# Norm boundaries: squares added on TensorE, residual terms for two blocks at once, modulation sums moved into the mixer

## What is computed

```python
c_act = jax.nn.silu(c)
for i in range(DEPTH):                          # DEPTH = 2
    mod = c_act @ ada_w[i] + ada_b[i]           # ada_w[i]: 1024 x 6144
    sh1, sc1, g1, sh2, sc2, g2 = jnp.split(mod[:, None, :], 6, axis=-1)
    h = rmsnorm(x, norm_g[i, 0]) * (1.0 + sc1) + sh1
    y = mlstm_mixer(h, ...) if i == 0 else sgu_mixer(h, ...)
    x = x + g1 * rmsnorm(y, norm_g[i, 1])
    h = rmsnorm(x, norm_g[i, 2]) * (1.0 + sc2) + sh2
    y = jnp.square(jax.nn.relu(h @ ffn_w1[i])) @ ffn_w2[i]
    x = x + g2 * rmsnorm(y, norm_g[i, 3])
```

## Time and profile before

| | us |
|---|---|
| median of 3 runs | 2249.4 |
| lowest, highest | 2245.52, 2251.71 |
| the profiled execution | 2242.23 |
| its span | 2240.4 |
| PE busy in it | 2130.8 |
| VectorE, ScalarE, POOL busy | 1230.7, 825.4, 96.0 |

### The profile page before, as it was taken

How to read it: one execution, slowest core, us unless ns; L and a number is a source line. 1 busy time by engine, 2 the same in 40 slices (tenths; PEclk the granted TensorE clock), 3 DMA queues, 4 the chain that set the end, 5 groups by cost and what they waited for, 6 DMA issues and landing times.

```text
span 2240.4 us, 29806 instructions
## 1 busy us (share of the span) xinstructions
PE 2130.8 (95%) x11614; PEld 1780.1 (79%) x11614; DVE 1230.7 (55%) x1994; ACT 825.4 (37%) x1229; POOL 96.0 (4%) x71
## 2 busy tenths in 40 slices
PE   6999879999998999999999999998989999999997
PEld 5897778888888998788888888884666689888886
DVE  4665766666667345647333336425557756536455
ACT  3433334334234222325242343334445534324243
POOL 0000010000001002401000000100000000000000
PEclk9999989999999999999999999999999999999998
DMA  9451314666551432231222222212011222222221
GB/s 292 152 187 38 114 58 152 205 210 198 192 188 57 149 97 91 79 116 52 94 94 94 94 94 90 68 61 87 1 48 54 70 95 75 94 95 94 94 84 66
DMA packets 224630, 239.34 MB, mean 107 GB/s; under 512 B 6642, under 2 KB 219021, under 8 KB 223877
## 3 DMA queue, kind: packets, MB, share of 16 engines
q1 hardware_dynamic: 182757, 193.73, 26.9%
q10 hardware_dynamic: 41760, 44.06, 6.0%
HBM read 230.81 MB, written 6.31 MB: 106 GB/s over the span
## 4 chain that ended last, share of the span: by engine, by line
PE 67%; issue 18%; DVE 7%; ACT 3%; DMA 3%; DVEq 1%; POOL 1%; SPq 1%; ACTq 0%; POOLq 0%
PE bank L544 43%; PE bank L1122 4%; PE bank L684 2%; PE bank L738 2%; DMA ada_raw<-in_ada_w 2%; PE bank L642 2%; PE bank L1070 1%; DVE ada_acc L1711 1%; PE bank L1059 1%; PE bank L1047 1%; PE bank L1011 1%; PE bank L1105 1%; PE bank L943 1%; PE bank L1093 1%; PE bank L609 1%
## 5 line engine op out<-in xcount | busy, mean ns | idle before, releaser
L1700 DVE TENSOR_TENSOR w_lo<-raw,w_hi 128x2048 fp32r<-128x2048 f32 x137 | 314.7, 2297 | 254.4 <-ACT w_hi L1190 254.2
L544 PE MATMUL bank<-h_hi,w_hi 128*128 128x512 f32 x1056 | 413.7, 392 | 0.0
L544 PE MATMUL bank<-h_hi,w_lo 128*128 128x512 f32 x1056 | 411.6, 390 | 0.0
L544 PE MATMUL bank<-h_lo,w_hi 128*128 128x512 f32 x1056 | 411.4, 390 | 0.0
L1190 ACT ACTIVATE w_hi<-raw 128x2048 fp32r<-128x2048 f32 x147 | 280.1, 1906 | 314.6 <-PE bank L544 307.9
L544 PE MATMUL bank<-g_hi,w_hi 128*128 128x512 f32 x688 | 271.4, 394 | 9.3 <-DVE g_lo L2483 5.1
L544 PE MATMUL bank<-g_hi,w_lo 128*128 128x512 f32 x688 | 269.5, 392 | 0.0
L544 PE MATMUL bank<-g_lo,w_hi 128*128 128x512 f32 x688 | 269.3, 391 | 0.0
L544 PEld LDWEIGHTS bank<-h_hi,w_lo 128*128 128x128 f32 x1056 | 198.5, 188 | 41.9
L544 PEld LDWEIGHTS bank<-h_hi,w_hi 128*128 128x128 f32 x1056 | 198.7, 188 | 40.8 <-issue 0.2
L544 PEld LDWEIGHTS bank<-h_lo,w_hi 128*128 128x128 f32 x1056 | 198.8, 188 | 40.7 <-issue 0.2
(11 more groups left out here) (415 smaller groups left out, 3677.8 us busy)
## 6 DMA issues: line engine op xcount, KB each, us to landing
raw<-in_ffn_w SPq DMA_DIRECT2D x64, 1024.0 KB, 5.2
ada_raw<-in_ada_w ACTq DMA_DIRECT2D x40, 1024.0 KB, 5.1
raw<-in_w_up SPq DMA_DIRECT2D x22, 1024.0 KB, 5.1
raw<-in_b_w_in SPq DMA_DIRECT2D x16, 1024.0 KB, 5.3
raw<-in_w_in SPq DMA_DIRECT2D x15, 1024.0 KB, 5.8
raw<-in_a_w_in SPq DMA_DIRECT2D x12, 1024.0 KB, 6.2
ada_head<-in_ada_w SPq DMA_DIRECT2D x8, 1024.0 KB, 12.0
raw<-in_b_w_out SPq DMA_DIRECT2D x8, 1024.0 KB, 5.2
```

Of the source, the lines that this page charges most:

```text
L544: mm = pe.matmul(o, x, y, start=(k == 0 and j == 0), stop=(k == kc - 1 and j == 2))
L1700: dve.tensor_tensor(w_lo[s][:], raw[s][:], f32(w_hi[s][:]), ALU.subtract).then_inc(sem("split_done"), 1)
```

## The change

`y_sum` is gone. PE adds the squares itself: `sums` takes `sqa` and the four `T[m]` as stationary operands, ten small matmuls where there were two. The second `rest_of` of a boundary is no longer cut around `variance`. `merge` makes the terms of two blocks (`TT`), then one addition over both (128x2x256) on VectorE in both halves; POOL adds nothing to x any more. ScalarE squares x two blocks at once, and PE takes them two, two and four at places of its own. In half 1 `diagonal` now stands ahead of the second piece of `rest_of`. Pieces 16 and 17 of the modulation are summed in the mixer's chunks 0 and 1, 18 and 19 during the first two tiles of `a_out`.

```diff
--- before.py
+++ after.py
@@ -180,6 +180,7 @@
...
+        TT = [at(f"tmp_pair{i}", "T", [P, 2, S], F32, i * 4096) for i in range(2)]
...
@@ -593,18 +594,21 @@
                 pe.matmul(RS[:] if out is None else out, ones[:], (diag if dg is None else dg)[:],
                           start=True, stop=True).then_inc(sem("rs_ready"), 1)
 
-            def sums(half, n, sq):
-
-                pe.wait_ge(sem(f"sq_ready{half}"), n + 1)
-                for c in range(2):
-                    mm = pe.matmul(bank[4 * half][:, c:c + 1], sq[:, half * HALF + c * P:half * HALF + c * P + P],
-                                   ones[:, 0:1], start=(c == 0), stop=(c == 1), skip_group_check=True)
+            def sums(half, name):
+
+                n = 12 * BOUNDS[name] + 4 + 4 * half
+                for i, sq in enumerate([sqa, T[0], T[1], T[2], T[3]]):
+                    pe.wait_ge(sem("y_squared"), n + max(i, 1))
+                    for c in range(2):
+                        mm = pe.matmul(bank[4 * half][:, c:c + 1], sq[:, half * HALF + c * P:half * HALF + c * P + P],
+                                       ones[:, 0:1], start=(i == c == 0), stop=(i == 4 and c == 1), skip_group_check=True)
                 mm.then_inc(sem(f"sq_used{half}"), 1)
 
             def x_sums(name, half, blocks):
 
                 for b in blocks:
-                    pe.wait_ge(sem(f"sq_ready{half}"), 9 * BOUNDS[name] + b + 2)
+                    if b % 2 == 0:
+                        pe.wait_ge(sem(f"sq_ready{half}"), 4 * BOUNDS[name] + b // 2 + 1)
                     for c in range(2):
                         mm = pe.matmul(bank[4 * half + 1][:, c:c + 1], xsq[:, b, c * P:c * P + P], ones[:, 0:1],
...
-                                sums(0, 9 * kb_, sqa)
+                                sums(0, name)
...
                             if two and (half, m, k) == (1, 3, 2):
-                                x_sums(name, 0, range(4, KB))
+                                x_sums(name, 0, range(4, 6))
+                            if two and (half, m, k) == (1, 3, 4):
+                                x_sums(name, 0, range(6, KB))
...
-                    sums(1, 9 * kb_, sqa)
+                    sums(1, name)
                 if (i, k) == (0, 7) and two or (i, k) == (1, 2) and not two:
                     spread_half(1, 2 * kb_)
                 if (i, k) == (1, 3) and two:
-                    x_sums(name, 1, range(3))
-                if (i, k) == (1, 6) and two:
-                    x_sums(name, 1, range(3, KB))
+                    x_sums(name, 1, range(2))
+                if (i, k) == (1, 5) and two:
+                    x_sums(name, 1, range(2, 4))
+                if (i, k) == (1, 7) and two:
+                    x_sums(name, 1, range(4, KB))
 
             def first_pair(name, t, q):
 
@@ -889,14 +897,15 @@
             t0, q0 = T0["a_out"], N0["a_out"] // 4
             pe.wait_ge(sem("mix_out"), 8 + 2)
             for i in range(2):
+                ada_mm(16 + i, i)
+            for i in range(2):
                 tile(t0 + i, i % 2, q0 + i // 2, g_hi, g_lo)
-                ada_mm(16 + i, i % 2)
+            ada_mm(18, 0)
             pe.wait_ge(sem("t5_in"), 48)
             pe.matmul(bank[6][0:WH, :], relb[:], onehot[:], start=True, stop=True).then_inc(sem("t5_mm"), 1)
 
             def last_ada():
-                for i in range(2, 4):
-                    ada_mm(16 + i, i % 2)
+                ada_mm(19, 1)
                 pe.wait_ge(sem("ada_added"), 1)
             last_pair("a_out", t0 + 2, q0 + 1, g_hi, g_lo, before_second=last_ada)
 
@@ -1222,14 +1231,12 @@
                 hs = [slice(half * HALF, half * HALF + HALF) for half in range(2)]
 
                 def x_squares(half):
-                    for b in range(KB):
-                        if half:
-                            act.wait_ge(sem("x_odd" if b % 2 else "x_even"), 4 * kb_ + b // 2 + 1)
-                            if b == 0:
-                                act.wait_ge(sem("sq_used0"), 9 * kb_ + 9)
-                        else:
-                            act.wait_ge(sem("x_ready0"), 8 * kb_ + b + 1)
-                        act.activation(xsq[:, b], X[:, b, hs[half]], ACT.Square).then_inc(sem(f"sq_ready{half}"), 1)
+                    for i in range(4):
+                        act.wait_ge(sem(f"x_ready{half}"), 4 * kb_ + i + 1)
+                        if half and i == 0:
+                            act.wait_ge(sem("sq_used0"), 9 * kb_ + 9)
+                        act.activation(xsq[:, 2 * i:2 * i + 2], X[:, 2 * i:2 * i + 2, hs[half]], ACT.Square)\
+                           .then_inc(sem(f"sq_ready{half}"), 1)
 
                 def split_next(s):
 
...
@@ -1399,11 +1406,13 @@
...
+            ada_in(17, 0, 17)
...
             squares(2)
...
             for i in range(2):
                 y_squares(i, [Y[:, 2 * i + b] for b in range(2)])
                 step_end(u0, i, q0)
-                ada_in(17 + i, 0, 17 + i)
-            ada_in(19, 0, 19)
+                if i == 0:
+                    ada_in(19, 0, 19)
             boundary("a_out", u0 + 1, q0 + 1, [Y[:, b] for b in range(4, KB)], 24)
 
             def ffn(name, ada, shift):
...
 
-                def y_sum(half, m):
-
-                    y_count[0] += 1
-                    dve.drain()
-                    dve.wait_ge(sem("y_squared"), y_count[0])
-                    i = dve.tensor_tensor(sqa[:, hs[half]], sqa[:, hs[half]], T[m][:, hs[half]], ALU.add)
-                    if m == 3:
-                        i.then_inc(sem(f"sq_ready{half}"), 1)
-
...
 
-                def merge(half, blocks):
-
-                    for b in blocks:
-                        t = T[2 + b % 2][:, hs[half]]
-                        if half and b > 1:
-                            dve.wait_ge(sem("x_odd" if b % 2 else "x_even"), 4 * kb_ + b // 2)
-                        i = dve.scalar_tensor_tensor(t, Y[:, b, hs[half]], y_gain_[:, b:b + 1], bank[4 * half][:, 0:HALF],
-                                                     ALU.mult, ALU.mult)
-                        if half and b % 2:
-                            i.then_inc(sem("x_term"), 1)
-                            continue
+                def merge(half):
+
+                    for i in range(4):
+                        t = TT[i % 2]
+                        for b in range(2):
+                            dve.scalar_tensor_tensor(t[:, b, hs[half]], Y[:, 2 * i + b, hs[half]], y_gain_[:, 2 * i + b:2 * i + b + 1],
+                                                     bank[4 * half][:, 0:HALF], ALU.mult, ALU.mult)
                         dve.drain()
-                        dve.tensor_tensor(X[:, b, hs[half]], X[:, b, hs[half]], t, ALU.add)\
-                           .then_inc(sem("x_even" if half else "x_ready0"), 1)
+                        x = X[:, 2 * i:2 * i + 2, hs[half]]
+                        dve.tensor_tensor(x, x, t[:, :, hs[half]], ALU.add).then_inc(sem(f"x_ready{half}"), 1)
 
                 def h_parts(half, blocks, after={}):
                     def rest(b):
@@ -1834,44 +1830,33 @@
...
-                y_out(0, 1)
-                y_sum(0, 0)
-                y_sum(0, 1)
-                y_out(0, 2)
-                y_sum(0, 2)
-                y_out(0, 3)
-                y_sum(0, 3)
-                rest_of(t2, 1, next_w[name][1], 2, lambda: variance(0, 9 * kb_ + 1))
+                for m in range(1, 4):
+                    y_out(0, m)
+                rest_of(t2, 1, next_w[name][1], 1)
+                y_count[0] += 8
+                variance(0, 9 * kb_ + 1)
                 diagonal(0, 2 * kb_)
                 spread_done(0, 2 * kb_)
                 if two:
-                    merge(0, range(KB))
+                    merge(0)
                     for m in range(3):
                         y_out(1, m)
-                    y_sum(1, 0)
-                    y_sum(1, 1)
...
                     variance(0, 9 * kb_ + 9, 1)
-                    y_sum(1, 2)
                     diagonal(0, 2 * kb_ + 1)
                     spread_done(0, 2 * kb_ + 1)
-                    h_parts(0, range(KB), {2: lambda: y_out(1, 3), 3: lambda: y_sum(1, 3),
+                    h_parts(0, range(KB), {2: lambda: y_out(1, 3),
                                            5: lambda: variance(1, 9 * kb_ + 1), 6: lambda: diagonal(1, 2 * kb_)})
                     spread_done(1, 2 * kb_)
-                    merge(1, range(KB))
-                    rest_of(t2 + 2, 0, (w_hi[0], w_lo[0]), 2, lambda: variance(1, 9 * kb_ + 9, 1))
-                    diagonal(1, 2 * kb_ + 1)
+                    merge(1)
+                    rest_of(t2 + 2, 0, (w_hi[0], w_lo[0]), 2, lambda: (variance(1, 9 * kb_ + 9, 1), diagonal(1, 2 * kb_ + 1)))
...
                     spread_done(1, 2 * kb_ + 1)
                 else:
                     h_parts(0, range(4))
                     y_out(1, 0)
...
+                    ada_sum(16, 0, ada_raw, (sem("ada_in"), 16 * 9))
...
```

(14 more changed lines are left out.)

6 lines of the change are left out of this document (1 added, 5 removed).

## The result

| | before | after |
|---|---|---|
| median of 20 runs, us | 2246.53 | 2252.89 |
| lowest, highest | 2237.22, 2251.71 | 2244.14, 2258.37 |
| span of the profiled execution | 2240.4 | 2251.5 |
| PE busy in it | 2130.8 | 2155.2 |

The changed kernel takes 1.0027 times as long, 95% interval 1.0018 to 1.0037: some 6 us slower. The change was forecast to gain 3.1 us. The time lies inside the forecast range and the ratio inside what the prediction called "within 0.3%", but with 20 runs on each side the interval excludes a gain: the sign was wrong. That the time itself lies inside the range is in part luck. The range was built on 2249.4 us, the median of 3 runs of the kernel before; 20 runs give 2246.53, and on that the same sum would have said 2243.4.

What follows compares the result with a forecast made beforehand. PE, busy 95%, was taken as the bound. Terms a_out -8.6, ffn0 +0.8, b_out +1.7, ffn1 +2.05, out2 +1.7 and four times -0.2 made -3.1: 2249.4 to 2246.3 us; 8-in-10 range 2238.5 to 2253.5.

Steps and rivals of the forecast that it cites:

- within 0.3%: Whole kernel: a change of under 6.7 us either way, not told from no change; chance 0.65.
- Modulation, -7.8: First boundary, a_out: pieces 16 and 17 summed in the mixer at no cost end PE's wait for piece 19, -7.8 us.
- The price of a small matmul, 0.107 us: `sums` on PE: 0.107 us per one-column matmul, sixteen more cost 1.71 us, ten times, 17 us more work.
- The rival of cheap small matmuls: `sums`: sixteen new records hold PE 0.4 us instead of 1.71, giving 2237.7 us; chance 0.03.
- What covers it in half 0: PE's old waits for sum and `diag` hide part of 1.71: ffn0 -0.4, b_out +0.5, ffn1 +0.85, out2 +0.6 us.
- h_lo's share: VectorE's shorter turns and the missing `y_sum` trim PE's small waits for h_lo: -0.2 us, four times.
- Half 1, +1.2: Half 1 of four two-norm boundaries: nothing covers the added 1.71 us; the missing fourth `y_sum` saves some 0.5: +1.2 us each.
- x for two blocks, diag ahead: Two-norm boundaries: a pair of blocks takes VectorE 1.54 us instead of 1.80; half 0 +0.2, half 1 net -0.2 us.
- the later lot of x's squares: Half 1 of the two-norm boundaries: the last lot of squares comes one step of k later, +0.4 us.
- a gain by the clock: Rival: fewer waits, split runs of x's squares; three of four clock falls go, -7.6 us or better, 2241; chance 0.22.
- the clock's case: Rival: new `sums` runs in half 1 bring falls, 1.7 us each; six give +7, 2256; chance 0.08 over 6.7 us slower.

Runs made afterwards that it cites:

- e11_diag: e1_ada with `diagonal` moved ahead of the second piece of `rest_of` in half 1; 2237.40 us, ratio 0.9961.
- e1_ada: The kernel before with only the modulation part of the change; 2241.65 us, ratio 0.9969.
- e2_ysum: The changed kernel with `y_sum` back on VectorE, `sums` at 4 records and the second `rest_of` cut again; 2237.39 us, ratio 0.9952.
- e4_light: The kernel before with each `sums` taking its small matmuls five times, 20 records instead of 4, same result; 2274.12 us, ratio 1.0121.
- e3_cut: The changed kernel with each `sums` cut in two, 12 records some steps of k earlier, then 8; 2248.13 us, ratio 1.0008.
- e10_fine: The changed kernel with each `sums` in five runs of 4 records at successive steps of k (out2's half 1: 8, then 12); 2242.89 us, ratio 0.9983.
- e7_lightcut: e4_light with the same number of small matmuls in two runs, 12 on the constants at an earlier place, then 8; 2258.76 us, ratio 1.0054.
- e9_pool: e2_ysum with POOL adding x's squares of blocks 0 to 5 in pairs, PE taking 20 records per half instead of 32; 2246.23 us, ratio 1.0000.

## Why the prediction was wrong, step by step

- **Modulation, -7.8.** Right: the wait of 7.28 is gone, the mixer keeps its length to 0.5 us, a_out up to its spread is 10.0 shorter for 10.1 forecast. Behind the spread a_out lost 2.3 again where 1.5 was forecast.
- **The price of a small matmul, 0.107 us.** Right: 20 records in 2.16 us in every `sums` that did not wait. The rival of cheap small matmuls fell, as the earlier trace rows said it would.
- **What covers it in half 0.** Right in the waits: 1.26, 0.28 and 0.23 for the sum and 0.86 for `diag` are gone in all four. In a table without the clock, each fall taken at 1.7 us, ffn0, b_out, ffn1 and out2 are +1.1, +1.2, +2.0 and +0.7, +5.0 together; the forecast, with h_lo's share, was 6.25 - 0.8 = +5.45.
- **Half 1, +1.2.** Measured: +1.8 to +2.0 us from the second to the third spread in each of four boundaries. The fall sets in between them: in b_out the last 12 matmuls up to the spread take 1030.99 - 1028.26 = 2.73 us, at 0.12 each it would be 1.4. So 1.3 of the 1.9 us there are the clock, and the work is left with some 0.6, half of the term. "Nothing covers the 1.71" was too dark: part of it falls into PE's small waits for h_lo (those of 0.34 and 0.27 us are gone).
- **x for two blocks, diag ahead.** The 1.54 us for a pair stands (four in 6.2 us in the trace), POOL's 0.70 too. `diag`'s place is right to 0.4 us: up to the last spread it was to give -0.9 without the later lot of x's squares and -0.5 with it. e11_diag, without the lot, measured -0.5 to -0.9 against e1_ada in each boundary, e2_ysum, with it, -0.4.
- **The clock, the step that failed.** The sum has no term for new falls of the clock, 0 us. It was a rival with much of the right mechanism ("as the runs of x_sums do now", six new falls, +7 us, 2256), a chance of about 0.2 for slower at all and of 0.08 for over 6.7 us; but it looked to half 1, beside h_lo's waits, and five of the ten falls came in half 0. There were ten new falls, one behind each `sums`, against some that went; net five in the four later boundaries, 5 x 1.7 = 8.5 us. The trace of before held this: four runs of 20 records, four falls behind them; four pairs of 16, one; the untouched run of 24, one. I read from it that falls are scattered and can go either way, and set a gain by the clock (0.22) above a loss. The right question was what PE had done just ahead of each fall, run length by run length. Had I taken a fall for likely behind each new run, the clock's case would have been the forecast; with the five net falls it is -3.1 + 8.5 = +5.4 us, and the boundaries show +5.7. That the two are so near is in part luck: a_out lost less to the clock than before (9.7 us of PE's work at 0.50 for 12.7), and the half-1 term was too high. By the table of the experiments the clock cost up to 8 us more than before and the rest came to -2.3.

The Trainium skill's page "TensorE: Matmul & The Clock Gate", Part 1: The HAM clock gate, names idle stretches of PE as what lowers the clock. The rows at 1003.46 and in out2 show a fall with no idle time at all, behind matmuls of one column. That page does not say how such matmuls count; here they did not keep the clock up.

**What stays open.** Whether a run's fall depends on more than the records ahead of it: of e4_light's ten runs two brought none. Which property of these matmuls matters was not tested: they have one column, are full fp32, and bring a new stationary operand each. All shares of the clock come from halving PE's busy time at 0.50 in one execution, or from means of the granted clock; they are estimates. How the loss behind half 1's last spread (small matmuls, then PE's waits of 0.67 and 1.9 us) would go was not found; neither shorter runs nor an earlier h touched it. And of the 4.3 us between the medians of e1_ada and e11_diag the spreads show 3; the rest is within the scatter.

## What to carry to other kernels

A small matmul on a full PE costs twice: its own 0.107 us, and, where many stand together, the clock for the matmuls behind them. So small ones go in groups of four or so between large ones, best where PE waits anyway, and ahead of each new group one looks in the trace what followed groups of that size before. A fall avoided at one place can come at the next, so what counts is PE's time at the lower clock in the whole stretch. Of this change the modulation part and `diag`'s place are worth keeping, together 5 to 12 us (e11_diag, 2237.4); the squares belong on VectorE, which had the time.

## What I had not expected of the hardware

- The clock went down with PE busy without a gap: in the changed kernel ten of ten `sums` of 20 one-column records were followed by 3.4 us at 0.50, nine of them with no wait inside the run; in e3_cut and e10_fine, outside a_out, none of those cut to 12, 8 or 4. But where a low stretch had begun before them, cut ones did not end it (17.1 us in e10_fine's ffn0).
- A POOL addition of 128x256 lengthened VectorE's of 128x512 from 0.69 to 1.17 us, and POOL's power beside VectorE's split took 1.62 us for 0.70.
- The clock in stretches that no edit touched differed from one execution to the next: before the mixer by up to 4.0 us of time, in the mixer by 4.7 from the kernel before (e1_ada, e7_lightcut and e9_pool lack one low stretch there). Kernels are compared by medians, or stretch by stretch.
